# Decoder step on one core: x transposes over four PSUM pairs, vectors of the last norm spread by products beside the last expert, its sums split over three engines

## What is computed

```
u   = x @ w_in + b_in                     # lru_x | lru_y | q | k | v | two gates
rec = scan(gates(conv4(lru_x))) * gelu(lru_y) @ w_lru_out
mix = (sigmoid(g_l) * rec + sigmoid(g_a) * att @ w_attn_out) @ w_o
x1  = LayerNorm(alpha * x + mix, ln1_g, ln1_b)
ff  = sum over the row's 2 of 32 experts: weight * (silu(x1 @ w_gate) * (x1 @ w_up)) @ w_down
y   = LayerNorm(alpha * x1 + ff, ln2_g, ln2_b)      # eps 1e-5, over 1024 columns
```

## Time and profile before

| what | value |
| --- | --- |
| timed runs | 1056.05, 1056.05, 1056.92 us; median 1056.05 |
| profiled execution | 1056.94 us, its span 1055.1 us |
| busy PE, DVE, ACT, POOL | 913.1, 419.8, 283.8, 128.2 us (87, 40, 27, 12% of the span) |
| DMA | 264.77 MB, 251 GB/s over the span |
| chain that ended last, by engine | PE 51%, SP's queue 19%, DMA 13%, DVE 11% |

### The profile page before, as it was taken

The page is one execution under the profiler, slowest core; times in us unless marked ns, Lnnn a source line. Parts: engine busy times, 40 slices in busy tenths (PEclk is TensorE's granted clock), DMA queues, the critical chain, the costliest instruction groups (busy, mean ns, idle before and its releaser), DMA issues.

```text
span 1055.1 us, 14518 instructions
## 1 busy us (share of the span) xinstructions
PE 913.1 (87%) x5905; PEld 625.0 (59%) x5905; DVE 419.8 (40%) x874; ACT 283.8 (27%) x531; POOL 128.2 (12%) x206
## 2 busy tenths in 40 slices
PE   4999999899999999999469999978777878778772
PEld 4989998898999989998433333323323323322220
DVE  3765867675656444532632112111111111111176
ACT  3667544444353422111401111101101101101121
POOL 2000300000000010030221211111111111100003
PEclk8999999889999999999769999999999999999975
DMA  9214722112212423265699999999999999999842
GB/s 286 96 54 89 190 84 70 59 41 81 81 42 80 87 81 81 80 263 217 240 391 426 420 422 423 422 420 425 423 421 423 423 421 423 423 421 423 338 165 81
DMA packets 86604, 264.77 MB, mean 251 GB/s; under 512 B 29291, under 2 KB 60151, under 8 KB 66026
## 3 DMA queue, kind: packets, MB, share of 16 engines
q1 hardware_dynamic: 79498, 248.56, 60.7%
q0 software_dynamic: 7040, 15.28, 3.9%
HBM read 258.98 MB, written 15.16 MB: 260 GB/s over the span
## 4 chain that ended last, share of the span: by engine, by line
PE 51%; SPq 19%; DMA 13%; DVE 11%; ACT 2%; issue 2%; POOL 1%; DVEq 0%; POOLq 0%; ACTq 0%
PE ps L782 29%; SPq L505 16%; DMA slot<-in_w_up 9%; PE ps L1078 9%; PE ps L1103 4%; SPq L508 3%; DMA raw<-in_w_o 2%; PE ps L908 1%; PE ps L874 1%; PE ps L898 1%; DMA st<-in_state_lru_h 1%; DVE hL L1535 1%; PE ps L1062 1%; DVE rawL L1454 1%; POOL zT L658 1%
## 5 line engine op out<-in xcount | busy, mean ns | idle before, releaser
L1078 PE MATMUL ps<-slot,xt 128*64 128x512 f32 x512 | 232.6, 601 | 40.3 <-DMA slot<-in_w_up 38.1
L1079 PE MATMUL ps<-slot,xt 128*64 128x512 f32 x512 | 233.2, 602 | 0.0
L1078 PEld LDWEIGHTS ps<-slot,xt 128*64 128x64 f32 x512 | 66.4, 138 | 177.8 <-issue 131.2
L782 PE MATMUL ps<-xTh,wh 128*128 128x260 f32 x704 | 147.7, 292 | 0.0
L782 PE MATMUL ps<-xTl,wh 128*128 128x260 f32 x704 | 143.9, 287 | 0.0
L782 PE MATMUL ps<-xTh,rawL 128*128 128x260 f32 x704 | 143.7, 286 | 0.0
L1103 PE MATMUL ps<-slot,hT 128*64 128x512 f32 x512 | 116.9, 597 | 29.2 <-issue 27.8
L1934 DVE TENSOR_TENSOR xt<-ps,g 128x512 f32<-128x512 f32 x32 | 22.1, 692 | 249.6 <-PE ps L1062 249.6
L1454 DVE TENSOR_TENSOR rawL<-raw,wh 128x1024 fp32r<-128x1024 f32 x68 | 84.1, 1241 | 87.1 <-ACT wh L1178 87.0
L782 PEld LDWEIGHTS ps<-xTh,wh 128*128 128x128 f32 x704 | 110.8, 193 | 5.9 <-issue 5.1
L782 PEld LDWEIGHTS ps<-xTl,wh 128*128 128x128 f32 x704 | 111.0, 193 | 0.0
(11 more groups left out here) (323 smaller groups left out, 1246.0 us busy)
## 6 DMA issues: line engine op xcount, KB each, us to landing
slot<-in_w_gate SPq DMA_DIRECT2D x64, 1024.0 KB, 29.8
slot<-in_w_up SPq DMA_DIRECT2D x64, 1024.0 KB, 32.1
slot<-in_w_down SPq DMA_DIRECT2D x32, 2048.0 KB, 33.3
raw<-in_w_in SPq DMA_DIRECT2D x18, 1024.0 KB, 5.2
raw<-in_w_in SPq DMA_DIRECT2D x16, 256.0 KB, 4.3
raw<-in_w_lru_out SPq DMA_DIRECT2D x4, 1024.0 KB, 4.8
raw<-in_w_attn_out SPq DMA_DIRECT2D x16, 256.0 KB, 4.5
raw<-in_w_o SPq DMA_DIRECT2D x4, 1024.0 KB, 5.1
```

Of the source, the lines that this page charges most:

```text
L782: last = mm(out_of[:, a, 0:HT], w[:, k, :], x[:, k, a * HT:(a + 1) * HT], start=(k == 0 and n == 0), stop=(k == KT - 1 and n == 2))
L1078: mm(out[0:CAP, :], tokens, w[:, q, :], start=start, stop=stop)
L1079: last = mm(out[CAP:P, :], tokens, w[:, 4 + q, :], start=start, stop=stop)
```

## The change

- The transposes of x go in turn into four pairs of banks (flat[n % 4]), and PE waits for DVE's split of a tile only from the fifth tile on. vectors_t stands behind projection tile 0 on PE. DVE's list is the same there.
- The four norm vectors are loaded as vec32, 32 partitions of 128 columns, ahead of load(10). A new function `spread` makes 16 products of 128 columns for two vectors: spread(0), for lnG and lnB, stands ahead of gate_up(31) on PE and ahead of the copies of expert 31 on ACT, which multiplies by ALPHA as it copies; spread(2), for ln2G and ln2B, stands behind the last down product.
- The last chunk comes in two halves, with a semaphore each; the down product of expert 31 waits for the second before its third group.
- The value that tells whether an extra block is needed is read at expert 2 by PE, ACT, DVE and POOL, and no longer at the end.
- In the tail "+ lnB" of m = 3 and 4 is POOL's. f0 + f1 is DVE's for m = 0, POOL's for m = 2, PE's for 1, 3 and 4. DVE makes x1 + ff and its total in one instruction (tensor_tensor_reduce, then a read of the accumulator, L2038) and scales the total to minus the mean; ACT squares with that as its bias and adds up (Square with accum_out), then takes the root. ACT normalises m < 3 in place, DVE multiplies them by ln2G, POOL adds ln2B. m = 3 and 4 are finished on DVE alone. Stores come from xr2.
- Two pairs of semaphores for stores of states are merged.

```diff
+FREE = (0, 1, 3, 7)
+BY_PE, BY_POOL = (1, 3, 4), 2
...
+            for n, name in enumerate(("ln1_g", "ln1_b", "ln2_g", "ln2_b")):
+                sp.dma_start(vec32[n * KT:(n + 1) * KT, :], A[name].rearrange("(k n) -> k n", n=P)).then_inc(s_l2, 16)
             load(10)
 
-            for n in range(RING, 3 * NE):
+            for n in range(RING, 3 * NE - 1):
                 load(n)
 
+            sp.wait_ge(*read_by(3 * NE - 1 - RING))
+            w_last = A["w_down"][NE - 1, :, :].rearrange("(p j) d -> p j d", p=P)
+            for h, signal in enumerate((s_wx[(3 * NE - 1) % RING], s_wl)):
+                sp.dma_start(slot[(3 * NE - 1) % RING][:, 4 * h:4 * h + 4, :].rearrange("p a b -> p (a b)"),
+                             w_last[:, 2 * h:2 * h + 2, :].rearrange("p j d -> p (j d)")).then_inc(signal, 16)
             sp.wait_ge(s_gup, NE - 2)
-            sp.wait_ge(s_x1o, 16 * TT)
-            for n, name in enumerate(("ln1_g", "ln1_b", "ln2_g", "ln2_b")):
-                sp.dma_start(vec4[n:n + 1, :], A[name].rearrange("(a n) -> a n", a=1)).then_inc(s_l2, 16)
...
-            for m, n in enumerate(ORDER[:-1]):
+            for m in (3, 4):
+                n = ORDER[m]
                 r = ROWS[n]
-                pool.wait_ge(s_l2, 68)
+                pool.wait_ge(s_xg, m - 2)
+                gp.tensor_tensor(xr2[n][0:r, :], xr2[n][0:r, :], lnB[0:r, :], ALU.add).then_inc(s_tp, 1)
...
+            n = ORDER[BY_POOL]
+            r = ROWS[n]
+            pool.wait_ge(s_x[n], 48)
+            gp.tensor_tensor(f0[n][0:r, :], f0[n][0:r, :], f1[n][0:r, :], ALU.add).then_inc(s_tp, 1)
+
+            for m, n in enumerate(ORDER[:-2]):
+                r = ROWS[n]
+                pool.wait_ge(s_vsp, 8)
                 pool.wait_ge(s_y2, m + 1)
-                if m == 1:
-                    pool.wait_ge(s_y3, 1)
-                if m >= 2:
-                    pool.wait_ge(s_yo[m % 2], 16 * (m // 2))
-                gp.tensor_tensor(y_out[m % 2][0:r, :], z2[m % 3][0:r, :], ln2B[0:r, :], ALU.add).then_inc(s_y3, 1)
+                gp.tensor_tensor(xr2[n][0:r, :], xr2[n][0:r, :], ln2B[0:r, :], ALU.add).then_inc(s_tp, 1)
 
...
-                if n >= 2:
-                    pe.wait_ge(s_xl, n - 1)
+                if n >= 4:
+                    pe.wait_ge(s_xl, n - 3)
                 for k in range(KT):
-                    last = nc.tensor.transpose(flat[n % 2][:, k * P:k * P + r], xrow[n][0:r, k * P:(k + 1) * P], ident[0:r, 0:r])
+                    last = nc.tensor.transpose(flat[n % 4][:, k * P:k * P + r], xrow[n][0:r, k * P:(k + 1) * P], ident[0:r, 0:r])
...
-            vectors_t()
             for step in STEPS:
                 what, args = step[0], step[1:]
                 if what == "tile":
                     tile(*args)
+                    if args[0] == 0:
+                        vectors_t()
...
                                   start=(q == 0), stop=(q == 3))
                 last.then_inc(signal, 1)
 
+            def spread(n0):
+
+                for g in range(2 * n0, 2 * n0 + 4):
+                    if n0:
+                        pe.wait_ge(s_vsp, g - 3)
+                    for k in range(4):
+                        last = mm(bank[FREE[g % 4]][:, k * P:(k + 1) * P],
+                                  ident[0:4 * KT, 4 * g + k:4 * g + k + 1].to_broadcast([4 * KT, P]), vec32[:, :],
+                                  start=True, stop=True)
+                    last.then_inc(s_mix, 1)
+
             def expert(e):
+                if e == NE - 1:
+                    pe.wait_ge(s_l2, 64)
+                    pe.wait_ge(s_xte, 2 * NE)
+                    pe.wait_ge(s_gue, NE - 1)
...
-            for m, n in enumerate(ORDER):
+            pe.wait_ge(s_ye, NE)
+            pe.wait_ge(s_vsp, 8)
+            for k, m in enumerate(BY_PE):
+                n = ORDER[m]
...
+            def spread(n0):
+
+                for g in range(2 * n0, 2 * n0 + 4):
+                    act.wait_ge(s_mix, g + 1)
+                    sc.activation(norms[g // 2][:, (g % 2) * 512:(g % 2 + 1) * 512], bank[FREE[g % 4]], ACT.Copy,
+                                  scale=1.0 if n0 else ALPHA).then_inc(s_vsp, 1)
...
+                sc.activation(sq[0:r, :], xr2[n][0:r, :], ACT.Square, bias=mv[0:r, m, 0:1],
+                              accum_out=mv[0:r, m, 1:2]).then_inc(s_sq, 1)
+                act.wait_ge(s_sq, m + 1)
+                sc.activation(mv[0:r, m, 2:3], mv[0:r, m, 1:2], ACT.Sqrt, scale=1.0 / D, bias=epsT[0:r, 0:1]).then_inc(s_sd, 1)
+
+            spread_of(0)
             for m in range(TT - 1):
-                normalise(m)
-                root_of(m + 1)
+                spread_of(m + 1)
+                if m < TT - 2:
+                    normalise(m)
...
+            dve.wait_ge(s_vsp, 4)
             dve.wait_ge(s_xr, 16 * TT)
-            dve.wait_ge(s_l2, 66)
             for m, n in enumerate(ORDER):
                 r = ROWS[n]
-                link(v.tensor_tensor(xr2[n][0:r, :], xr2[n][0:r, :], lnG[0:r, :], ALU.mult))
-                v.tensor_tensor(xr2[n][0:r, :], xr2[n][0:r, :], lnB[0:r, :], ALU.add).then_inc(s_xw, 1)
-
-            dve.wait_ge(s_tabo, 1)
-            n_over = dve.value_load(ovT[0:1, NOV:NOV + 1], min_val=0, max_val=NOV)
+                ins = v.tensor_tensor(xr2[n][0:r, :], xr2[n][0:r, :], lnG[0:r, :], ALU.mult)
+                if m >= 3:
+                    ins.then_inc(s_xg, 1)
+                else:
+                    link(ins)
+                    v.tensor_tensor(xr2[n][0:r, :], xr2[n][0:r, :], lnB[0:r, :], ALU.add).then_inc(s_xw, 1)
...
-            def stats2(m):
+            def summed(m):
...
+                r = ROWS[n]
+                if m < 3:
+                    dve.wait_ge(s_xw, m + 1)
+                else:
+                    dve.wait_ge(s_tp, m - 2)
+                if m in BY_PE:
+                    dve.wait_ge(s_mix, 8 + BY_PE.index(m) + 1)
+                    rows_sum = flat[BY_PE.index(m) % 2][0:r, :]
+                elif m == BY_POOL:
+                    dve.wait_ge(s_tp, 3)
+                    rows_sum = f0[n][0:r, :]
...
+                link(v.tensor_tensor_reduce(out=xr2[n][0:r, :], in0=xr2[n][0:r, :], in1=rows_sum, scale=1.0, scalar=0.0,
+                                            op0=ALU.add, op1=ALU.add, accum_out=mv[0:r, m, 0:1]))
+                v.tensor_scalar(mv[0:r, m, 0:1], mv[0:r, m, 0:1], -1.0 / D, None, ALU.mult).then_inc(s_z, 1)
...
+                n = ORDER[m]
+                r, z = ROWS[n], xr2[n]
                 dve.wait_ge(s_z, TT + m + 1)
...
+                link(v.scalar_tensor_tensor(out=zc[m % 2][0:r, :], in0=z[0:r, :], scalar=mv[0:r, m, 0:1], in1=ln2G[0:r, :],
+                                            op0=ALU.add, op1=ALU.mult))
...
-            stats2(0)
-            factors(0)
+            summed(0)
             for m in range(TT - 1):
-                stats2(m + 1)
-                if m + 1 < TT - 1:
-                    factors(m + 1)
-                scale2(m)
+                summed(m + 1)
+                if m:
+                    scale2(m - 1)
+                if m < TT - 2:
+                    factors(m)
+            finish(TT - 2)
             finish(TT - 1)
```

More of the change, by code:

```diff
@@ L1117, in _ @@
                 expert(e)
+                if e == 2:
+                    pe.wait_ge(s_tabo, 1)
+                    n_over = pe.value_load(ovT[0:1, NOV:NOV + 1], min_val=0, max_val=NOV)
             down(NE - 1)
-            pe.wait_ge(s_l2, 64)
-            pe.wait_ge(s_gue, NE)
-            for n in range(4):
-                if n >= 2:
-                    pe.wait_ge(s_l2, 64 + n - 1)
-                pick = ident[0:4, n:n + 1].to_broadcast([4, P])
-                for h in range(2):
-                    last = mm(pair[n % 2][:, h, :], pick, vec4[:, h * 512:(h + 1) * 512], start=True, stop=True)
-                last.then_inc(s_mix, 1)
-            pe.wait_ge(s_tabo, 1)
-            n_over = pe.value_load(ovT[0:1, NOV:NOV + 1], min_val=0, max_val=NOV)
+            spread(2)
             with pe.If(n_over > 0):
@@ L1392, in _ @@
                 expert(e)
+                if e == 2:
+                    act.wait_ge(s_tabo, 1)
+                    n_over = act.value_load(ovT[0:1, NOV:NOV + 1], min_val=0, max_val=NOV)
             scale_out(NE - 1)
[L1394 to L1400 removed]
+            spread(2)
             with act.If(n_over > 0):
```

137 lines of the change are left out of this document (61 added, 76 removed).

## The result

The kernel after took 1044.8 us (median of 4 runs, 1043.58 to 1046.65), the kernel before 1056.49 (4 runs, 1056.05 to 1057.71): ratio 0.9887, 95% interval 0.9873 to 0.9900. The direction was right, the size was not. The two traces show three terms that were wrong: the start by its sign, the end behind DVE, which was taken for a constant, and the price of the sixteen products. The profiled execution of the kernel after was the slowest of its four, 1046.65 us.

What follows compares the result with a forecast made beforehand. It took full DMA engines to bound the middle, packed PE before it, and DVE the tail. Span 1055.1 − 8.1 (tail) + 2.1 (start) = 1049.1, + 0.95 = 1050.0 us; range 1045.5 to 1054 (8 in 10).

Steps and rivals of the forecast that it cites:

- The start, +2.1: Start of the program: conv(0) on DVE at 31.9 in place of 29.84, making PE late by 2.1 us.
- tile 0 begins at about 19.8, when the split is done: Start on PE: the first projection tile waits for DVE's split of the first weights, beginning at 19.8 in place of 21.09.
- by 30: Start on DVE: the prediction named itself wrong if conv(0) started by 30 us; it expected 31.9.
- four PSUM pairs gain nothing: Start on PE: four pairs for the transposes of x gain 0, since tile 0 waits for the first weights.
- The 6.8 us behind it ... I leave them as they are: End, behind DVE's last operation: last store and end of the program, 6.8 us, taken as unchanged.
- 0.9, and at most 3: PE ahead of expert 31: us for the sixteen products of 128 columns, covered by PE's waits; at most 1.5 if uncovered.
- DVE's start 5.4 us earlier: Tail: DVE starts at 1002.9, when the x1 rows land, 5.4 us earlier than before.
- POOL and DVE exclude each other: Tail: a DVE operation with two inputs in SBUF and a POOL addition hold each other; without it −12.6, not −8.1.
- rival 2: Tail: POOL's additions don't hold DVE, so the end is 1035.7 and the time 1045.6 us; chance 0.08.
- The sums of tiles 2 to 4 are hidden: Tail: these f0 + f1 sums, wanted from 1022 on, at 4.3 us each on PE, cost nothing.
- −8.1: Tail: DVE's last operation ends at 1040.2 in place of 1048.28, 8.1 us earlier.
- rival 3: Tail: the sum with its total costs double, so −5.3 there with +2.1 at the start, time 1052.9 us; chance 0.10.

Runs made afterwards that it cites:

- e3: Kernel before with the vectors' transposes behind projection tile 0 and the transposes of x over four pairs of banks: 1053.4 us, ratio 0.9978 to before.
- e4: Kernel after with the vectors' transposes ahead of projection tile 0 again: 1047.59 us, ratio 0.9919 to before.
- e1: Kernel before, unchanged, run once more: one time, 1059.12 us.
- e5: Kernel before with its fourth tile (m = 3) finished on DVE alone, so POOL makes three additions and not four: 1053.18 us against 1057.25, ratio 0.9965.
- e2: Kernel before with one edit, the vectors' transposes behind projection tile 0: 1055.65 us against 1056.44, ratio 0.9992.
- e10: Kernel after with the two additions of lnB (m = 3 and 4) on DVE and not on POOL: 1047.16 us, ratio 0.9918 to before.
- e13: Same kernel as e10, run again in another job: 1044.47 us, ratio 0.9879 to before.
- e12: e11 with the two additions of lnB on DVE also: 1042.92 us, ratio 0.9869 to before.
- e11: Kernel after with the first sixteen products in four groups in PE's waits and m = 2 finished on DVE alone: 1043.01 us, ratio 0.9881 to before.
- e6: Kernel after with its third tile (m = 2) finished on DVE alone: 1042.31 us, ratio 0.9869 to before.
- the control: Kernel after, unchanged, run again in the third job: 1043.94 us, ratio 0.9885 to before.
- e15: e12 with DVE waiting for each x1 row tile by itself and not for all five: 1041.15 us, ratio 0.9860 to before.
- e16: e15 with f0 + f1 of m = 1 on DVE and not on PE: 1039.93 us, ratio 0.9833 to before.
- e8: Kernel after with the first sixteen products in four groups, each where PE waits for a chunk: 1045.42 us, ratio 0.9903 to before.

## Why the prediction was wrong

- **The start, +2.1: measured −2.7 (trace), −3.0 by medians (e3), −3.4 by ratios (e4).** The step that failed is "tile 0 begins at about 19.8, when the split is done". In the trace of before the split ended at 19.8 and the vectors landed at 19.46, by chance nearly together: one of the sixteen parts of the first weights landed at 17.46, the others by 14.02 (e1: all by 11.97). In twelve other traces they were all there by 12.03. I took the split for the usual limit. The earlier trace rows had the answer: PE's 6.29 us ended with the vectors' DMA, and that wait is what the change removes. With it fell three more: "I take the rise to stay near 24.8" (with tile 0 the clock's rise came earlier too: 0.50 over 14.6 to 19.7, 1.00 from 19.9), the queue behind DVE's wait, which hides behind the second piece of the weights (23.79), so that conv(0) starts at 27.16 where "by 30" was named as a sign of being wrong, and "four PSUM pairs gain nothing", against which e3's median speaks, within the noise. The transposes of the vectors, priced at 0.3, took 0.81 and cost nothing.
- **"The 6.8 us behind it ... I leave them as they are": −2.7 there.** They were POOL's drain, not a constant. This step had no row: the chain of waits ends with DVE's last operation, since it doesn't show drains. The sum ran along DVE, and the end hung on POOL's last addition, which the change drops (e5: −4.1 from that alone).
- **The sixteen products, "0.9, and at most 3" and "at most 1.5": 3.73 to 5.05 us, and the last down product 0.6 to 4.1 us behind the last chunk**, where it is 0.6 to 0.9 in the traces of before, e1, e2, e3 and e5. I priced them by columns. Each is two passes, and each pass has a weight load of its own (32 in the trace): 0.23 us a product at a granted clock of 1.00. That alone fits into PE's waits (e4, e10); what was not priced is the fall of the clock, which came in five of seven traces, and in none of the five with the products in four groups.
- **DVE's start 5.4 us earlier: right.** 10.68 us behind the last chunk before, 5.14 after. From there to its end I had 37.3 us: it is 37.4 in e4, where the clock stayed up, and 39.8 in the trace of after, which holds the 3.69 us of waiting for PE.
- **The sum with its total, 1.28 + 0.25: right** (1.22, a read of 0.08, a scaling of 0.15). The table load: 1.28, as taken. The halves of the last chunk: nothing, since the last down product still waits 1.39 us for hT.
- **POOL and DVE exclude each other: right**, and rival 2 with it wrong: operations with two inputs in SBUF take 1.94 and 3.04, and one that reads PSUM takes 1.22 at 1026.55 beside POOL's 2.35. The Trainium skill, page "SBUF — State Buffer", section "Who interferes with whom", says the same: a DVE instruction with two SBUF inputs contends with a GpSimd instruction that reads SBUF, one with at most one SBUF input (outside DVE's two-port modes) does not. The price was not what I made of it: two additions taken off POOL gained nothing (e10, e13, and e12 against e11).
- **"The sums of tiles 2 to 4 are hidden": wrong for PE's first sum**, which is now m = 1: 6.5 us, most of it at a granted clock of 0.50, and 3.69 us of DVE's time. The 4.3 was the mean of two, of which the first took 5.1. This wait goes with the fall of the clock ahead of it, which delays the last down product and with it the f rows: it is 3.69, 3.76 and 5.27 us where the clock fell while the products ran (after, e6, e13), 2.07 in the control, 0.14 in e4 and nothing in e10. Forecast for DVE's end were 42.5 us behind the last chunk; after had 44.9, its control 43.3, and e4 42.75.

Put together: −2.7 and −2.7 where +2.1 and 0 stood, and −5.7 (after) to −7.3 (its control) where −8.1 stood for the tail. That the total came out only 0.7 us below the range is luck: the tail gave less than its term, the start and the end gave 4.8 and 2.7 us more. No run takes the new statistics (the sum with its total, Square) alone; that they are worth their share of the −8.1 is read from the rows, and from DVE's 37.4 us.

Two slips in the recorded sum change nothing in this: 1017.9, 1.28 and 0.25 make 1019.4 and not 1019.2, and a reduce of 2.56 for three of the five tiles gives 1044.0 and not 1043.0, so rival 3 stood at 1053.9.

## What to carry to other kernels

Where an engine waits for two things that end nearly together, the trace of one execution doesn't say which of them is the usual limit; read what each waits for, and how its parts landed, before pricing the removal of one. Look behind the last operation of the chain: there the end can hang on an engine that the chain leaves out, and then the last small instruction of that engine can be worth more than a faster chain. Small products that fill a gap are better spread over several gaps: it kept the clock up in five traces of five, though no run shows that it alone saves time.

## What the runs showed of the hardware

- POOL's closing drain ended 7.69 or 7.70 us after its last addition in all 18 traces of this case, whether that addition took 2.35 us or some 3.25. Where it was the latest, the span ended 0.22 or 0.23 us behind it; in the six others (e5, e6, e11, e12, e15, e16) 3.02 to 3.04 us behind DVE's last operation.
- The granted clock fell to 0.50 while PE was busy for 4.88 of 5 us with sixteen products of 32 rows by 128 columns. With the sixteen in one piece it fell beside them or within 1 us behind them in five traces of seven; in four groups between larger products it stayed at 1.00 in five of five.
- One or two of the sixteen parts of a transfer at the start can be late: the last part of the first weights landed at 11.7 to 12.0 us in 13 of the 18 traces, at 14.4 to 14.5 in four (e2, e4, e5, e8), and at 17.46 in one of the kernel before.
